# A two-layer decoder trunk on one core: in both layers the last row tile's scaled rows for the experts are made by GpSimd in two operations instead of by VectorE in one

## The reference: what is computed

```python
def rms_norm(x, g):
    x32 = x.astype(jnp.float32)
    y = x32 * lax.rsqrt(jnp.mean(x32 * x32, axis=-1, keepdims=True) + EPS)
    return (y * g.astype(jnp.float32)).astype(x.dtype)
...
        h = h + mix
        h = h + grouped_moe(rms_norm(h, norm_ffn[i]), w_router, w_gate_e[i], w_up_e[i], w_down_e[i])
```

## Time and profile before

| what | before |
|---|---|
| median of 3 runs | 1133.27 us (1133.26 to 1133.99) |
| the profiled execution's own time | 1134.14 us |
| its span, first to last instruction | 1131.9 us |
| granted TensorE clock, mean | 0.998 |
| PE busy | 1107.4 us, 98% |
| DVE busy | 894.3 us, 79% |
| ACT busy | 749.9 us, 66% |
| POOL busy | 131.2 us, 12% |

### The profile page before, as it was taken

One profiled execution on the slowest core, in us unless ns is written; L12 is line 12 of the kernel. 1 busy time (PEld: TensorE's weight loads), 2 busy tenths in 40 slices (PEclk: granted clock), 3 DMA queues, 4 the chain that ended last, 5 costly groups with the idle time before them and its releaser, 6 DMA issues.

```text
span 1131.9 us, 16852 instructions
## 1 busy us (share of the span) xinstructions
PE 1107.4 (98%) x5722; PEld 886.0 (78%) x5722; DVE 894.3 (79%) x1226; ACT 749.9 (66%) x957; POOL 131.2 (12%) x91
## 2 busy tenths in 40 slices
PE   9999999999999999999999999999999999999996
PEld 7888878757888888888788866776888888888785
DVE  6483777368999999998966479637999999999886
ACT  7483322347878787788565469436787878787765
POOL 0000000011212212120000000001221212221000
PEclk9999999999999999999999999999999999999999
DMA  9473213336999999998851210433999999999632
GB/s 368 171 279 149 94 47 135 154 120 245 358 390 372 383 372 386 377 377 348 324 202 44 106 38 20 168 112 138 339 366 384 377 386 373 391 371 382 262 136 75
DMA packets 50595, 286.28 MB, mean 253 GB/s; under 512 B 9321, under 2 KB 9597, under 8 KB 21358
## 3 DMA queue, kind: packets, MB, share of 16 engines
q1 hardware_dynamic: 37086, 250.93, 57.6%
q0 software_dynamic: 13456, 34.65, 8.3%
HBM read 271.38 MB, written 30.41 MB: 267 GB/s over the span
## 4 chain that ended last, share of the span: by engine, by line
PE 86%; DVE 7%; ACT 4%; issue 1%; DMA 1%; ACTq 0%; DVEq 0%; POOLq 0%
PE psum L569 81%; PE psum L938 2%; DVE arena L2659 2%; ACT whi L1383 2%; DMA arena<-vscr,cur 1%; DVE arena L2672 1%; PE psum L979 1%; DVE wlo L1942 1%; PE psum L849 1%; ACT ahi L1383 1%; DVE h L2493 0%; DVE h L2500 0%; DVE wlo L1938 0%; DVE h L2486 0%; PE psum L655 0%
## 5 line engine op out<-in xcount | busy, mean ns | idle before, releaser
L1938 DVE TENSOR_TENSOR wlo<-raw,whi 128x2048 fp32r<-128x2048 f32 x200 | 456.1, 2289 | 69.8 <-ACT whi L1383 59.5
L569 PE MATMUL psum<-whi,ahi 128*128 128x512 f32 x1088 | 433.6, 400 | 2.7 <-ACT ahi L1383 2.1
L569 PE MATMUL psum<-wlo,ahi 128*128 128x512 f32 x1088 | 422.8, 390 | 0.8 <-DVE wlo L1942 0.8
L569 PE MATMUL psum<-whi,alo 128*128 128x512 f32 x1088 | 418.3, 391 | 0.0
L1383 ACT ACTIVATE whi<-raw 128x2048 fp32r<-128x2048 f32 x200 | 382.8, 1916 | 41.7 <-PE psum L569 41.7
L569 PEld LDWEIGHTS psum<-whi,ahi 128*128 128x128 f32 x1088 | 204.3, 188 | 49.2 <-issue 4.5
L569 PEld LDWEIGHTS psum<-whi,alo 128*128 128x128 f32 x1088 | 204.2, 188 | 43.7
L569 PEld LDWEIGHTS psum<-wlo,ahi 128*128 128x128 f32 x1088 | 204.5, 188 | 40.0 <-DVE wlo L1942 1.2
L1383 ACT ACTIVATE arena<-psum 128x512 f32<-128x512 f32 (+3 forms) x150 | 83.3, 565 | 109.0 <-PE psum L569 77.9
L1383 ACT ACTIVATE ahi<-psum 128x512 fp32r<-128x512 f32 x146 | 81.8, 594 | 102.8 <-PE psum L938 39.3
L2767 POOL DMA_INDIRECT arena<-vscr,cur x32 | 69.5, 2172 | 386.1 <-DVE cur L2379 370.9
(11 more groups left out here) (222 smaller groups left out, 894.5 us busy)
## 6 DMA issues: line engine op xcount, KB each, us to landing
raw<-w_moe_dram SPq DMA_DIRECT2D x192, 1024.0 KB, 8.8
raw<-w_dense_dram SPq DMA_DIRECT2D x34, 1024.0 KB, 8.8
yscr<-arena POOLq DMA_DIRECT2D x2, 4096.0 KB, 24.3
arena<-yscr SPq DMA_DIRECT2D x6, 1024.0 KB, 6.8
vscr<-arena POOLq DMA_DIRECT2D x8, 512.0 KB, 2.9
h<-x_dram SPq DMA_DIRECT2D x4, 512.0 KB, 7.5
arena<-w_proj_dram POOLq DMA_DIRECT2D x2, 1024.0 KB, 6.9
arena<-yscr SPq DMA_DIRECT2D x4, 512.0 KB, 4.4
```

Of the source, the lines that this page charges most:

```text
L569: return nc.tensor.matmul(o, l, r, start=start, stop=stop, **kw)
L1938: tt(wlo[:, b % SPL, :], raw[:, b % RAW, :], halves(whi[:, b % SPL, :]), ALU.subtract).then_inc(lo_ready, 1)
```

## The change

In `norm_x`, for the last tile of the two norms ahead of the experts, DVE now makes only the reciprocal. `row_root[n]` remembers how far `v_link` has counted by then, as a constant. POOL, ahead of its fourth store, waits for the gain, for the store of tile 1 (the same buffer), for `h` and for that reciprocal, and makes the row in two operations: a tensor_scalar (`h` times the reciprocal) and, behind a wait for its own first operation, a tensor_tensor (times the gain). `m["xz"]` counts one more, so the wait for the second memset goes from 2 to 3.

```diff
@@ DVE, norm_x
                 q = n * TB + tb
                 dve.wait_ge(n_root, q + 1)
+                if n in FFN and tb == TB - 1:
+                    link(nc.vector.reciprocal(st[:, q, 2:3], st[:, q, 1:2]))
+                    row_root[n] = chain[0]
+                    return
                 link(nc.vector.reciprocal(st[:, q, 2:3], st[:, q, 1:2]))
@@ POOL, the stores of the rows
                 n = 1 + 3 * layer
                 for tb in range(TB):
+                    if tb == TB - 1:
+                        q = n * TB + tb
+                        pool.wait_ge(s_gain, 16 * SCALED[n])
+                        pool.wait_ge(s_rows[tb - 2], 16 * layer + 16)
+                        pool.wait_ge(h_ready, (n - 1) * TB + TB)
+                        pool.wait_ge(v_link, row_root[n])
+                        nc.gpsimd.tensor_scalar(out=xn(q), in0=h[:, tb, :], scalar1=st[:, q, 2:3],
+                                                scalar2=None, op0=ALU.mult).then_inc(m["xz"], 1)
+                        pool.wait_ge(m["xz"], 2)
+                        nc.gpsimd.tensor_tensor(xn(q), xn(q), area(AR_GAIN, D), ALU.mult)\
+                            .then_inc(n_xn, 1)
                     pool.wait_ge(n_xn, nrows(n, tb))
                     pool.dma_start(vscr[layer][tb * P:(tb + 1) * P, :], xn(n * TB + tb))\
                         .then_inc(s_rows[tb], 16)
@@ POOL, gather
-                        pool.wait_ge(m["xz"], 2)
+                        pool.wait_ge(m["xz"], 3)
```

More of the change, by code:

```diff
@@ L224, in build @@
         n_rec = sem("n_rec")
+        row_root = {}
         p_ready = sem("p_ready")
```

## The result

Over 9 executions each, the changed kernel took 1137.11 us in the median (1136.29 to 1141.98), the kernel before 1133.47. The medians differ by 3.64 us, 0.32%. The ratio on record, 1.0038 with a 95% interval of 1.0029 to 1.0047, is not the quotient of the medians; either way the change is a loss, small and clear of noise. The prediction was 1137.6 us, 4.3 us above the median that it started from. The profiled execution took 1136.73 us, with a span of 1134.6. Two executions of the later groups, one of e6 with 4755 us and one of the kernel before with 6209 us, were disturbed by something unknown and count in no ratio.

What follows compares the result with a forecast made beforehand. PE was taken as the bound, busy 98% of the span. Per layer, holds of 0.2 and 2.3 us less 0.2 lead and 0.15 slack gave 2.15; twice, 4.3 on 1133.27 gave 1137.6 us, range 1133.4 to 1139.8.

Steps and rivals of the forecast that it cites:

- The lead that the removal gives: DVE's routing chain, without the last row, would start 0.2 us earlier in each layer.
- PE's slack: At PE's weight load for the ranks, a filling matmul lets the mask come about 0.15 us later without delaying PE.
- POOL's lengths: POOL's tensor_scalar would take 1.1 us (bounds 0.97 to 1.78), its tensor_tensor 2.2 us (bounds 1.78 to 2.59).
- That POOL's arithmetic holds DVE's two-input operations too: In the routing chain, POOL's two operations would shut out DVE's two-input operations as well as its tensor_scalars.
- Which operation is held, and for how long: Routing chain: L2305 held 0.2 us by POOL's tensor_scalar, a later two-input operation 2.3 us by its tensor_tensor.
- The 0.24 us that I had added: Extra hold of DVE beyond the POOL instruction's length, taken from L2346 beside a memset; partly included in the 2.3 us.
- My rule: A POOL operation that reads SBUF locks DVE's tensor_scalars and two-input operations out for its whole length.
- the second hold: In the routing chain, POOL's tensor_tensor holds DVE's next two-input operation for 2.3 us in each layer.
- The sum: PE later by 2.15 us in each of two layers, 4.3 us in all.
- Rival 4: PE's stop of about 2.2 us lowers its clock, costing a few us more; chance 0.06 together with rival 3.
- Rival 3: POOL's first arithmetic starts late; 6 us late would give about 1140 us; chance 0.06 together with rival 4.
- Rival 2: In the routing chain DVE goes first and POOL waits: 1133.1 to 1133.5 us, not slower; chance 0.07.

Runs made afterwards that it cites:

- e6: Changed kernel with POOL's two operations in the other order, tensor_tensor (gain) first, then tensor_scalar (reciprocal): 1139.16 us, ratio 1.0044.
- e3: Kernel before, with the last tile's row for the experts cut to 16 elements on DVE and nothing added on POOL: 1133.74 us, ratio 1.0000.
- e1: Changed kernel with the held DVE tensor_scalar (rank below 1.5) made as a two-input operation that multiplies with ones: 1137.14 us, ratio 1.0037.
- e9: Changed kernel with POOL's gain product moved ahead of tile 2's store and the mask's tensor_scalar made two-input with ones: 1134.69 us, ratio 1.0009.
- e7: Changed kernel with POOL's tensor_tensor before its tensor_scalar and the mask's DVE tensor_scalar made two-input with ones: 1136.75 us, ratio 1.0027.
- e10: Changed kernel unaltered, run again for more executions and a second profile: 1138.15 us over 6 executions, ratio 1.0038.
- e2: Changed kernel, but DVE waits for POOL's finished row before its first routing operation: 1146.39 us, ratio 1.0114.
- e5: Changed kernel with six small DVE operations added as probes while POOL's tensor_scalar runs: one execution, 1141.68 us.
- e8: Changed kernel with POOL's gain product moved ahead of tile 2's store, the reciprocal product behind that store: 1135.80 us, ratio 1.0019.

## Why the prediction was right, step by step

- **The lead that the removal gives**, put at 0.2 us: it is 0.06. L2308 starts 0.50 us behind the start of the last logits matmul (243.15 against 242.65); L2303 started 0.56 behind it. The logits were signalled later than I had put it. In e3, with the last row cut down to 16 elements, the same distance is 0.43 (243.35 against 242.92), a lead of 0.13. PE gets nothing from it, as forecast; e3 measured that directly.
- **PE's slack**, put at 0.15 us: the mask is later by (249.75 − 242.65) − (248.23 − 243.06) = 1.93 us, PE by 1.67, so 0.26.
- **POOL's lengths**, put at 1.1 and 2.2 us: 2.86 and 2.35. The tensor_tensor was well sized; the tensor_scalar was mis-sized by far, outside my bounds of 0.97 to 1.78, which came from memsets. That a one-tensor operation with a scalar from memory is the longer of the two, no row of before could say.
- **That POOL's arithmetic holds DVE's two-input operations too**: shown by e1 and e6 for the tensor_tensor, which makes the whole loss here. For the tensor_scalar e6 to e9 show it only at its start, and only for L2324, a bf16 operation that does 256 elements in 0.29 us where L2320 on float32 takes 0.42. Whether its start would hold a two-input operation on float32 is not shown; L2321 in e6 and e7 passed. The step was right where it mattered, and the trace of the change alone would have spoken against it.
- **Which operation is held, and for how long**: I put 0.2 us by the first and 2.3 us by the second. In the trace the first holds nothing, since its holding part, some 1.1 us from 242.54 on, is just over when L2310 comes at 243.66; the second holds L2333 for 1.98 and 1.90 us. The 0.24 us that I had added behind POOL's end are not there: the hold ends 0.04 us behind it, and in the earlier trace rows too L2346 ends 0.03 us behind the memset, so what it had more than the memset's length lay ahead of the memset.
- **Where two errors cancel, which is luck**: the tensor_scalar is 1.76 us longer than I had it, and it holds for its first 1.1 us and its end in place of its whole length. My rule with the true length would have held L2310 from 243.66 to 245.40, 1.74 us, with the second hold on top. That is about 1.74 + 1.98 − 0.06 − 0.26 = 3.4 us for each layer, 1140.1 in all (an estimate from these rows), above the end of my range. What carries the result is the second hold, and that one doesn't depend on when POOL gets to it: the tensor_tensor began 2.83 us behind the last logits matmul in place of my 1.14, and DVE's next operation was in its way all the same.
- **The sum**, 2.15 us for each layer: with the measured terms it is 1.98 − 0.06 − 0.26 = 1.66, and PE shows 1.67 and 1.60. The forecast 4.3 us was 1.0 too much for an execution at a steady clock, and 0.7 too much for the medians.
- **Rival 4, the clock**, was held for unlikely at a stop of 2.2 us, because PE stood for longer at the end of the program before the clock fell. That reading was wrong: e10 shows a fall behind 1.44 us, in one layer of two. It costs 1.5 us there (8.75 against 7.27) and 1.3 to 2.0 in e2. It explains times near 1138.5, but not the first nine's median: 1137.11 was taken at a mean clock of 0.998, like the fastest. For the executions at 1140.35 and 1141.98 no profile was taken. Two falls as in e10 reach about 1139.5 to 1140. The mean clock on record is 0.996 for the first and 0.993 for the second, the lowest of the nine, so the clock has a part in them; a longer fall, as in e2's layer 1, would fit, but is not shown.
- **Rival 3** (POOL's first arithmetic starts late) did not happen: the tensor_scalar starts 0.13 us behind the store ahead of it (242.54 after 241.88 + 0.53).
- **Rival 2** (DVE goes first) is seen on a small scale: POOL's operations were stretched by 0.13 to 0.44 us when they met a DVE operation already running (e5, e6, e8).

## What to carry to other kernels

Work that is moved from VectorE to GpSimd is not off VectorE's path while both work on SBUF: here 1.28 us of work, all but some 0.1 of it hidden, became a hold of 2 us in a chain that PE waits for. Look at what VectorE does while GpSimd would compute, and at which kinds of operations it does then. Before moving anything, ask what the removal alone is worth; a cut to 16 elements (e3) answers that in one run, and here the answer was nothing. A short new stop of PE can also cost more than its length, by its clock.

## What the runs showed of the hardware that I had not expected

- GpSimd's tensor_scalar of 128x1024 floats with a scalar from memory takes 2.86 us beside an idle VectorE (e2) as in the changed kernel, its tensor_tensor 2.35, its memset 0.97. Where they met a VectorE operation already running they took up to 3.30 and 2.79 (e6, e8).
- The tensor_scalar does not hold VectorE for its whole length. In about its first 1.1 us a tensor_scalar (e5) and a two-input operation on bf16 (e6 to e9) are held, in the middle (1.2 to 1.7 us in, by the probes of e5) neither kind, and from 0.78 us before its end a tensor_scalar (e6), while a two-input one on float32 (e7) and one on bf16 (L2325 in the changed kernel, 0.48 us before the end) pass. The Trainium skill's SBUF — State Buffer (the section on the engine and DMA sides) says that the pair is held for the whole instruction. For the tensor_tensor that agrees (e6: held until its end), for the tensor_scalar the measurement differs and decides. The last part behaves like the memset of the earlier trace rows. That it is a pass of reading, one of computing and one of writing would fit, but is not shown.
- The clock fell behind a stop of 1.44 us in one case and not behind 1.51 us in the same execution (e10). There PE had resumed at 774.83, the clock fell within 776 to 777, stood at 1.2 GHz until within 779 to 780, and came back while PE worked.
